# Scaling x by rows ahead of its transposes, and running the norm units eight at a time, in a hybrid attention layer step

## What is computed

```
mod = silu(c) @ w_ada + b_ada            # shift, scale, gate, for each of 9 batch entries
h = rmsnorm(x, ln_gain) * (1 + scale) + shift
proj = h @ w_in                          # q_a, ckv, krope, g_a, q_b, k_b, v_b, q_i, k_i, w_i, g_b
o_a = latent attention(q_a, ckv, krope)  # 8 heads, chunk-causal
o_b = sparse attention(q_b, k_b, v_b, top-k of an indexer on q_i, k_i, w_i)
y = concat(rmsnorm(o_a) * silu(g_a), rmsnorm(o_b) * silu(g_b))
out = rmsnorm(x + gate * (y @ w_out))    # and the new rows of the caches are outputs too
```

## Time and profile before

| | |
|---|---|
| median of 3 runs | 901.76 us (901.02 to 901.81) |
| profiled execution | 901.86 us |
| its span | 900.1 us |
| TensorE busy (matmuls) | 869.3 us, 97% |
| VectorE busy | 440.8 us, 49% |
| ScalarE busy | 335.4 us, 37% |
| DMA over the span | 190.07 MB, mean 211 GB/s |

### The profile page before, as it was taken

The page is one execution under the profiler, slowest core; times in us unless marked ns, Lnnn a source line. Parts: engine busy times, 40 slices in busy tenths (PEclk is TensorE's granted clock), DMA queues, the critical chain, the costliest instruction groups (busy, mean ns, idle before and its releaser), DMA issues.

```text
span 900.1 us, 14070 instructions
## 1 busy us (share of the span) xinstructions
PE 869.3 (97%) x5686; PEld 766.5 (85%) x5686; DVE 440.8 (49%) x910; ACT 335.4 (37%) x624; POOL 125.7 (14%) x207
## 2 busy tenths in 40 slices
PE   3998999999999999999999999999999999999996
PEld 2776778899999988888899989988999998888886
DVE  3523433443744314444455467364465466677262
ACT  3324334244443333332333354233244336554252
POOL 0000002110210000013241300000212123530000
PEclk9999999999999999999999999999999999999999
DMA  9999976855444334357463486655798733894313
GB/s 369 356 404 418 387 266 184 261 186 176 155 147 141 106 108 150 119 154 245 163 189 120 124 284 231 231 190 193 266 326 275 270 114 111 304 280 131 128 63 124
DMA packets 50352, 190.07 MB, mean 211 GB/s; under 512 B 7632, under 2 KB 8264, under 8 KB 45040
## 3 DMA queue, kind: packets, MB, share of 16 engines
q1 hardware_dynamic: 35280, 141.35, 44.2%
q0 software_dynamic: 14864, 47.30, 16.4%
q10 hardware_dynamic: 144, 0.52, 0.1%
HBM read 178.55 MB, written 12.69 MB: 212 GB/s over the span
## 4 chain that ended last, share of the span: by engine, by line
PE 89%; DVE 3%; ACT 3%; DMA 2%; issue 2%; SPq 0%; DVEq 0%; ACTq 0%
PE proj L2043 32%; PE proj L2033 30%; PE proj L2084 2%; PE bankO L2014 2%; PE proj L2014 2%; PE bankS L2043 1%; PE bankO L2168 1%; PE bankS L2084 1%; PE bankO L2180 1%; DMA araw<-in_ada_pairs 1%; PE bankT L2043 1%; DMA raw<-in_units 1%; PE bankO L2007 1%; PE bankS L2237 1%; ACT w_hi L1080 1%
## 5 line engine op out<-in xcount | busy, mean ns | idle before, releaser
L1449 DVE TENSOR_TENSOR w_lo<-raw,w_hi 128x1024 fp32r<-128x1024 f32 (+3 forms) x166 | 195.9, 1186 | 214.1 <-ACT w_hi L1080 213.0
L1080 ACT ACTIVATE w_hi<-raw 128x1024 fp32r<-128x1024 f32 (+3 forms) x168 | 168.3, 1006 | 169.5 <-PE proj L2033 92.6
L2043 PE MATMUL proj<-hT_hi,w_hi 128*128 128x384 f32 x576 | 198.0, 344 | 0.0
L2043 PE MATMUL proj<-hT_hi,w_lo 128*128 128x384 f32 x576 | 193.0, 335 | 0.0
L2043 PE MATMUL proj<-hT_lo,w_hi 128*128 128x384 f32 x576 | 192.8, 335 | 0.0
L2033 PE MATMUL proj<-w_hi,hT_hi 128*128 128x512 f32 (+2 forms) x458 | 174.4, 381 | 3.7 <-DVE hT_lo L1542 2.6
L2033 PE MATMUL proj<-w_hi,hT_lo 128*128 128x512 f32 (+2 forms) x458 | 171.3, 374 | 0.0
L2033 PE MATMUL proj<-w_lo,hT_hi 128*128 128x512 f32 (+2 forms) x458 | 171.1, 374 | 0.0
L2043 PEld LDWEIGHTS proj<-hT_hi,w_hi 128*128 128x128 f32 x576 | 108.2, 188 | 9.3 <-issue 7.7
L2043 PEld LDWEIGHTS proj<-hT_lo,w_hi 128*128 128x128 f32 x576 | 108.2, 188 | 0.1
L2043 PEld LDWEIGHTS proj<-hT_hi,w_lo 128*128 128x128 f32 x576 | 108.1, 188 | 0.0
(11 more groups left out here) (403 smaller groups left out, 1181.8 us busy)
## 6 DMA issues: line engine op xcount, KB each, us to landing
raw<-in_units SPq DMA_DIRECT2D x181, 512.0 KB, 4.0
araw<-in_ada_pairs SPq DMA_DIRECT2D x32, 1024.0 KB, 8.6
wuvT<-in_w_uv_t POOLq DMA_DIRECT2D x8, 512.0 KB, 6.7
kcT<-in_dsa_k_t POOLq DMA_DIRECT2D x8, 512.0 KB, 6.0
vc<-in_cache_dsa_v POOLq DMA_DIRECT2D x8, 512.0 KB, 5.1
gate_scratch<-stage POOLq DMA_DIRECT2D x8, 384.0 KB, 4.0
raw<-in_units SPq DMA_DIRECT2D x8, 336.0 KB, 3.5
raw<-in_units SPq DMA_DIRECT2D x8, 320.0 KB, 4.9
```

Of the source, the lines that this page charges most:

```text
L1080: return nc.scalar.activation(out, in_, func, scale=scale, **kw)
L1449: V.tensor_tensor(w_lo[:, SLOT[u], 0:w], raw_of(u)[:, 0:w], high(u)[:, 0:w].bitcast(F32), ALU.subtract).then_inc(lo_ready, 1)
L2043: ins = mm(banks[blk][:, 0:TOK], w[:, n, cols], a[:, kt, :], start=first and n == m == 0, stop=final and n == per - 1 and m == 2)
```

## The change

x is scaled in place by its row factors before it is turned: ScalarE takes columns 0 to 1023, VectorE 1024 to 2047, in three pieces each (`xs`). `rb`, `xdiag` and `rbc` are gone; the turns now wait for the scaled halves and go through x row tile by row tile (t = i // 4). The evictions of the turned blocks are plain copies, of bank T on VectorE and of bank S on ScalarE. Four turns stand behind unit 1, six behind unit 3, and the last two inside `first_unit`, ahead of row tile 2; `first_unit` does tiles 0 and 1 pass by pass. The first splits (`w0`) move behind `modT` 0 on ScalarE and into `h` 0 on VectorE.

The unit list of the opening is written anew. `ah` 1 runs in two runs of four, `ada` 1 to 3 in two runs of eight each; two or three projection units stand between the runs, and two behind each turn (the turn's own unit included). At the units of `TURNS` ScalarE and VectorE do the turn's steps ahead of the splits that stand in the same row. `osq` 7 moves from the row of unit 166 to that of unit 165. All units keep their content; the steps that are placed by the end of `ada` 3 (`ld_small`, `ld_const`, `bias`, `ld_uvT` and so on) come one or two units earlier.

```
-    out = a + key[:1] + b[:2] + g0[:1] + b[2:5] + one + b[5:]
+    out = a + key[:1] + b[:4] + one + b[4:]
     b = of("ada", 1)
-    out += two[:1] + b[:4] + key[1:2] + b[4:7] + two[1:] + b[7:10] + g0[1:2] + b[10:13] + three + b[13:]
+    out += two[:1] + g0[:1] + b[:8] + key[1:2] + two[1:] + b[8:]
     b = of("ada", 2)
-    out += one_b[:1] + b[:4] + key[2:3] + b[4:8] + g0[2:3] + b[8:12] + key[3:4] + b[12:14] + one_b[1:] + b[14:]
+    out += g0[1:2] + three + b[:8] + key[2:3] + one_b + b[8:]
     b = of("ada", 3)
-    out += two_b[:1] + b[:4] + key[4:5] + b[4:7] + g0[3:4] + b[7:10] + key[5:6] + b[10:13] + two_b[1:] + b[13:]
-    out += g1[:1] + key[6:] + g0[4:] + g1[1:] + g2
+    out += g0[2:3] + key[3:4] + b[:8] + key[4:5] + two_b[:1] + key[5:6] + b[8:]
+    out += g0[3:4] + two_b[1:] + key[6:] + g1[:1] + g0[4:] + g1[1:] + g2
...
-    put(0, ("xsq", 0), ("xsq", 1), ("xsq", 2), ("xr", 0))
-    put(1, ("rb", 0))
-    for n in range(6):
-        put(1 + n + 3 * (n > 4), ("xT", n), ("xS", n))
+    put(0, ("xsq", 0), ("xsq", 1), ("xsq", 2), ("xr", 0), ("xs", 0), ("xs", 1), ("xs", 2))
+    for n, u in enumerate((1, 1, 3, 3, 3)):
+        put(u, ("xT", n), ("xS", n))
 
     for n, ch in enumerate(MODS):
         u = LAST_UNIT[ch] + (n > 0)
         if n == 0:
-            put(u, ("w0", 0), ("busy", 1), ("modT", 0), ("busy", 5))
-            put(u + 1, ("h", 0), ("hl", 0), ("w1", 0))
+            put(u, ("busy", 1), ("modT", 0), ("w0", 0), ("busy", 5))
+            put(u + 1, ("h", 0), ("hl", 0), ("w1", 0), ("xT", 5), ("xS", 5))
...
-    run(u, "osq", 8)
+    run(u, "osq", 7)
+    put(u + 6, ("osq", 7))
...
+        def xs(t):
+
+            act.wait_ge(sem("x_rstd"), 1)
+            half = x_sb[:, t, 0:D // 2]
+            copy(half, half, scale=stat[:, 12 + t:13 + t]).then_inc(sem("x_lo_scaled"), 1)
+
+        def xS(n):
+
+            t, g = (2 * n + 1) // 4, (2 * n + 1) % 4
+            filled(act, "xS", n)
+            copy(xsT[:, 4 * g:4 * g + 4, P * t:P * (t + 1)],
+                 bank["S"][:].rearrange("p (k q) -> p k q", q=P)).then_inc(free["S"], 1)
...
-            copy(high(FIRST)[:, 512:UCOL], raw_of(FIRST)[:, 512:UCOL]).then_inc(hi_ready, 1)
...
+                copy(high(FIRST)[:, 512:UCOL], raw_of(FIRST)[:, 512:UCOL]).then_inc(hi_ready, 1)
...
-            for v in splits(u):
-                split(v)
+            if u not in TURNS:
+                for v in splits(u):
+                    split(v)
             if last_unit(u) and CHUNKS[c][0] not in ("wo", "gate"):
                 evict(c, u)
             for name, n in PLAN[u]:
                 if name in steps:
                     steps[name](n)
+            if u in TURNS:
+                for v in splits(u):
+                    split(v)
...
-            link(V.reciprocal(stat[:, 12:15], stat[:, 12:15]))
-            dve.wait_ge(sem("eye_in"), 16)
-            for t in range(NT):
-                V.tensor_scalar(xdiag[:, t, :], eye[:], stat[:, 12 + t:13 + t], None,
-                                ALU.mult).then_inc(sem("xs_ready"), 1)
-
-        def rb(n):
-            filled(dve, "rb", n)
-            V.tensor_copy(rbc[:], bank["S"][:, 0:TOK]).then_inc(free["S"], 1)
-
-        def turned(kind, n, b, i):
-
-            t, g = i % NT, i // NT
-            emptied(dve, "rb", 0)
-            filled(dve, kind, n)
-            V.tensor_tensor(xsT[:, 4 * g:4 * g + 4, P * t:P * (t + 1)], bank[b][:].rearrange("p (k q) -> p k q", q=P),
-                            rbc[:, P * t:P * (t + 1)].unsqueeze(1).broadcast_to([P, 4, P]),
-                            ALU.mult).then_inc(free[b], 1)
+            V.reciprocal(stat[:, 12:15], stat[:, 12:15]).then_inc(sem("x_rstd"), 1)
+
+        def xs(t):
+
+            dve.wait_ge(sem("x_rstd"), 1)
+            half = x_sb[:, t, D // 2:D]
+            V.tensor_scalar(half, half, stat[:, 12 + t:13 + t], None, ALU.mult).then_inc(sem("x_hi_scaled"), 1)
 
         def xT(n):
-            turned("xT", n, "T", 2 * n)
-
-        def xS(n):
-            turned("xS", n, "S", 2 * n + 1)
+
+            t, g = 2 * n // 4, 2 * n % 4
+            filled(dve, "xT", n)
+            V.tensor_copy(xsT[:, 4 * g:4 * g + 4, P * t:P * (t + 1)],
+                          bank["T"][:].rearrange("p (k q) -> p k q", q=P)).then_inc(free["T"], 1)
...
-        def w0(_):
-            dve.wait_ge(hi_ready, 1)
-            V.tensor_tensor(w_lo[:, SLOT[FIRST], 0:512], raw_of(FIRST)[:, 0:512], high(FIRST)[:, 0:512].bitcast(F32),
-                            ALU.subtract).then_inc(lo_ready, 1)
-
         def h(m):
 
             dve.wait_ge(sem("mod_ready"), m + 1 if m < 2 else m // 2 + 2)
-            emptied(dve, "xT", 5 if m > 1 else 1)
-            emptied(dve, "xS", 5 if m > 1 else 0)
+            emptied(dve, "xT", 5 if m > 1 else 4)
+            if m > 1:
+                emptied(dve, "xS", 5)
             if m == 0:
 
                 for kt in range(2):
-                    ins = V.tensor_scalar(h_first[:, kt, :], xsT[:, kt, 0:SEQ], modT[:, 1, kt, 0:1],
-                                          modT[:, 0, kt, 0:1], ALU.mult, ALU.add)
-                link(ins)
-                for kt in range(2):
-                    if kt:
-                        dve.wait_ge(hi_ready, 2)
-                        V.tensor_tensor(w_lo[:, SLOT[FIRST], 512:UCOL], raw_of(FIRST)[:, 512:UCOL],
-                                        high(FIRST)[:, 512:UCOL].bitcast(F32), ALU.subtract).then_inc(lo_ready, 1)
+                    links[0] += 1
+                    V.tensor_scalar(h_first[:, kt, :], xsT[:, kt, 0:SEQ], modT[:, 1, kt, 0:1],
+                                    modT[:, 0, kt, 0:1], ALU.mult, ALU.add).then_inc(chain, 1)
+                    dve.wait_ge(hi_ready, kt + 1)
+                    cols = slice(512 * kt, 512 * (kt + 1))
+                    V.tensor_tensor(w_lo[:, SLOT[FIRST], cols], raw_of(FIRST)[:, cols], high(FIRST)[:, cols].bitcast(F32),
+                                    ALU.subtract).then_inc(lo_ready, 1)
+                    dve.wait_ge(chain, links[0])
...
-            for t, n in ((0, 0), (1, 0), (0, 1), (1, 1), (2, 0), (2, 1)):
-                rows = slice(P * t, P * (t + 1))
-                if t == 0:
-                    pe.wait_ge(sem("hT_hi_ready"), n + 1)
-                    pe.wait_ge(hi_ready, n + 1)
-                if t == 2:
-                    pe.wait_ge(sem("hT_hi_ready"), 2 + MORE)
-                mm(banks[t][:], hT_hi[:, n, rows], hi_[:, n, :], start=n == 0, stop=False)
-                if t == 0:
-                    pe.wait_ge(lo_ready, n + 1)
-                mm(banks[t][:], hT_hi[:, n, rows], lo_[:, n, :], start=False, stop=False)
-                if t == 0:
-                    pe.wait_ge(sem("hT_ready"), n + 1)
-                if t == 2:
-                    pe.wait_ge(sem("hT_ready"), 2 + MORE)
-                ins = mm(banks[t][:], hT_lo[:, n, rows], hi_[:, n, :], start=False, stop=False)
+            for tiles in ((0, 1), (2,)):
+                if 2 in tiles:
+                    xT(5)
+                    xS(5)
+                for n in range(2):
+                    whole = MORE if 2 in tiles else 0
+                    pe.wait_ge(sem("hT_hi_ready"), (2 if whole else n + 1) + whole)
+                    for a, w, start in ((hT_hi, hi_, n == 0), (hT_hi, lo_, False), (hT_lo, hi_, False)):
+                        if w is lo_:
+                            pe.wait_ge(lo_ready, n + 1)
+                        elif a is hT_lo:
+                            pe.wait_ge(sem("hT_ready"), (2 if whole else n + 1) + whole)
+                        else:
+                            pe.wait_ge(hi_ready, n + 1)
+                        for t in tiles:
+                            ins = mm(banks[t][:], a[:, n, P * t:P * (t + 1)], w[:, n, :], start=start, stop=False)
...
-        def rb(n):
-            pe.wait_ge(sem("xs_ready"), NT)
-            mm(take("rb", n, "S")[:, 0:TOK], ones[:], xdiag[:].rearrange("p t q -> p (t q)"), start=True,
-               stop=True).then_inc(full["S"], 1)
-
         def turn(kind, n, b, i):
 
-            t, g = i % NT, i // NT
-            pe.wait_ge(sem(f"x_in{t}"), 16)
+            t, g = i // 4, i % 4
+            pe.wait_ge(sem("x_lo_scaled" if g < 2 else "x_hi_scaled"), t + 1)
```

More of the change, by code:

```diff
@@ L594, in program @@
     c_cols = at("c_cols", 80, [P, 9 * KT])
-    xdiag = at("xdiag", 82, [P, NT, P])
-    rbc = at("rbc", 86, [P, TOK])
     relb = at("relb", 88.5, [P, HEADS])
@@ L1166, in h @@
             act.wait_ge(sem("mod_ready"), m + 1 if m < 2 else m // 2 + 2)
-            emptied(act, "xT", 5 if m > 1 else 1)
-            emptied(act, "xS", 5 if m > 1 else 0)
+            emptied(act, "xT", 5 if m > 1 else 4)
+            if m > 1:
+                emptied(act, "xS", 5)
             if m == 0:
@@ L1364, in kl @@
                  bank["T"][:].rearrange("p (h s) -> p h s", s=P)).then_inc(free["T"], 1)
```

(8 more changed lines are left out.)

1 line of the change is left out of this document (added), and 2 rows, old and new, of the table STEP_BANKS.

## The result

The changed kernel takes **908.64 us** (median of five, 906.07 to 911.13) against 901.76 us before: ratio 1.0079, 95% interval 1.0056 to 1.0101. It is slower, as forecast, but by 6.9 us and not by 1.8, and it is 2.1 us above the wide range of the forecast (899.5 to 906.5) and 3.1 above its own (901.7 to 905.5). The profiled execution is the slowest of the five (911.13 us, span 909.3), so single times from it lie up to 2.5 us late by the end. The five executions also differ more than those of the kernel before do, and their mean granted clock goes with it: 0.994 to 0.995 in the two shortest, 0.987 to 0.990 in the other three.

A forecast was written before the change was run, and what follows sets the result against it. TensorE bounds the kernel, with DMA nearly even in the opening; -1.9 - 2.5 - 3.5 + 8.6 + 2.7 - 1.5 = +1.9, along the path +1.8 us: 903.6 us, own range 901.7 to 905.5, wide 899.5 to 906.5.

The forecast's parts named there:

- the price of the waits: New `araw` waits inside runs of eight, counted at 8.6 and 2.7 us, with usual unit lengths behind them.
- TensorE slows after the waits: Rival: each of three or four new waiting stretches brings a slow start of 1 to 1.5 us; 907 to 909 us; chance 0.08.
- Unit 10 ends at 34.8, 1.9 us earlier: Opening, up to the second unit of `ah` 1: the scaled x saves 1.9 us (bounds 1.0 and 2.9).
- x is scaled beside other work: Opening: scaling done by 17.3 us on ScalarE and 16.8 on VectorE, beside the first norm units and turns.
- New waits of 8.6 and 2.7 us for `araw`: Runs of eight: 8.6 us of waits up to `ada` 2 k8, then 2.4 to 3.1 more, taken as 2.7.
- The hole and the pair of `ada` 3 k6: Load queue dry near 87 to 91 us; that pair lands 17.5 to 18.2 us after the run's start, wanted at 15.1.
- The old waits at the turns, -3.5 us: Turns: steps ahead of the splits remove TensorE's waits, 2.6 us for `hT_lo` and 0.85 for `modT`.
- `osq` 7, -1.5 us: Near 530 us: the last square one row earlier removes TensorE's 1.51 us wait for `ysum` (bounds 0 and -1.5).
- TensorE's own work behind unit 10, -2.5 us: Behind unit 10: fewer separate norm runs and fewer projection units following them save 2.5 us (bounds 1.4 and 3.2).
- The rate, 0.41 MB/us: Loads in the opening move at 0.4095 MB/us, against 0.49 asked by a cycle with a run of eight.

The follow-up runs named there:

- the kernel with filled gaps: The changed kernel plus 38 small products of ones ahead of the nine norm-unit pairs where TensorE waited: 904.74 us, ratio 1.0029.
- the kernel with eight places ahead: The changed kernel with projection loads put eight places ahead of their units in the load order instead of six (`AHEAD` 8): 898.79 us, ratio 0.9963.
- the two halves above: Two runs: the changed kernel with the old unit list, 898.32 us; the kernel before with the new unit list alone, 909.88 us.
- the new order only: The kernel before with the new unit list and nothing else of the change: 909.88 us, ratio 1.0096.
- the edit alone: The kernel before with only the turn's steps put ahead of the splits on ScalarE and VectorE: 900.69 us, ratio 0.9984.
- the kernel with half columns: The changed kernel, loading only half of each norm unit's columns on all 128 partitions from each slot's second use on: 892.41 us, ratio 0.9891.

## Why the prediction was right in its sign and wrong in its size

The forecast was 903.6 us, the result 908.64: 5.0 us. **The step that failed is the price of the waits.** The sum put a wait for `araw` at its own length and the products behind it at their usual lengths, and the clock at nothing. The mechanism was named, as the rival "TensorE slows after the waits", with 907 to 909 us, and given a chance of 0.08. It was the right one: filled gaps gave 3.9 us back, and the kernel with filled gaps, 904.74, is 1.1 us from the forecast.

That the rival's figure holds 908.64 is in part luck: it counted three or four places of 1 to 1.5 us, from the first 32 matmuls, whose windows show the clock at 1.00; measured were two places of 2.9 us in the slowest execution, at 0.50.

The argument against the rival was that the waits of up to 1.5 us at the turns had no slow unit behind them. At the turn near 70 us of the kernel before they read:
```profile
71.91 1.93 PE L2014 MATMUL bankO<-araw,cs 128*32 128x256 f32 x32 [0.85 <-DVE modT L1497]
75.34 0.47 PE L2033 MATMUL proj<-w_hi,hT_hi 128*128 128x512 f32 x1 [1.50 <-DVE hT_lo L1542]
```
Those were two waits, 0.85 and 1.50 us, with 1.93 us of matmuls between them, and the granted clock stayed at 1.00 (TensorE busy 5.65 of the 8 us from 70 to 78). A run of eight gives two or three waits of up to 1.4 us with 1.1 us of small matmuls between them, and there the clock fell in most cases, though not in all: TensorE was busy 2.87 of 5 us at 45 to 50, where the clock fell to 0.86 on the mean, and 1.93 of 5 us in the kernel with eight places ahead of its stretch at 0.66. The prediction took one harmless case for the rule. Its own numbers said that the new waits are another case: some 8.6 us in three runs whose norm units take 0.43 us each. That should have given the rival far more than 0.08, or a term in the sum: 2.9 us at a place (0.9 for two norm units and 2.0 for the `kb` unit).

The prediction named the Trainium skill ("TensorE: Matmul & The Clock Gate", Part 1) for this rival: idle time brings the low rate, and sustained work wins back the full one. The trace agrees in that the price was paid behind the waits (6.33 us for 4.33 at a clock of 0.50 to 0.63). That waits this short, with matmuls between them, are enough is what these runs add.

Point by point:

- *Unit 10 ends at 34.8, 1.9 us earlier*: right. It ended at 34.7 or so, though the first landing was 0.35 us later than in the kernel before. Alone the scaled x is worth some 1.6 us. Its lead moved the landing of `ada` 2 k6 forward too, as the path of the prediction had it, and was lost behind that (see the two halves above).
- *x is scaled beside other work*: right; 17.4 and 16.3 us against 17.3 and 16.8. VectorE took 0.69 us for 1024 columns, less than the bound of 0.96. `modT` 0 came 1.6 us earlier, for 1.7.
- *New waits of 8.6 and 2.7 us for `araw`*: right in sum, 11.0 measured for 11.3, and the landing of `ada` 2 k6 at 76.46 for 76.2. This is the mechanism and no luck: by 76.46 us 29.1 MB were moved (381 GB/s), for the 29.35 worked out. From the same landing the prediction counted 11.8 us to `ada` 2 k8; it took 14.6, of which 2.9 are the two slow pieces.
- *The hole and the pair of `ada` 3 k6*: right in kind. The hole is at 87 to 92 us, for 87 to 91. The pair landed at 110.65, 19.6 us behind the run's start for 17.5 to 18.2. SyncE's three issues of projection loads took 3.12 us there where one usually takes 0.43, and the three pairs behind them 1.87 for 1.0 (0.33 each), so this pair was issued 2.7 us later than by the usual durations. Two other runs bear on it: with filled waits the last pair was issued 4.1 us behind the run's start and landed at 18.4, with the new order only 5.0 and 18.5; here it was 5.9 and 19.6. That fits, but no run changed only the issues.
- *The old waits at the turns, -3.5 us*: the waits went. With the old order the edit alone gave 1.6 us, since 1.0 us of waits for `araw` came in their place: the loads were even with TensorE before the change, as the first part of the prediction says. In the new order the waits for loads are a term of their own, and the kernel with half columns fits the full 3.5.
- *`osq` 7, -1.5 us*: 1.2 us by its median, the wait gone: right within the error.
- *TensorE's own work behind unit 10, -2.5 us*: not tested apart. The kernel with half columns, which is the change without its waits, came out at 892.41 for the 892.4 worked out, so the terms of saved work hold in sum; errors that cancel between them are not ruled out.
- *The rate, 0.41 MB/us*: right; 405 to 429 GB/s in the windows shown in which the queue was full. No wait was taken away by a higher rate.

What the prediction did not ask at all is whether `LOADS` still fits the new unit list. `AHEAD` was left at 6 by the change, and that alone is 9.9 us.

## What to carry to other kernels

When a run of small work outpaces its loads, look at three things apart: the waits (11.0 us here), the slow matmuls behind repeated short waits (3.9 us by the medians), and the place of each load in the queue, which decides how many of both there are (`AHEAD` 8 took away 4.2 us of waits and most slow matmuls, 9.9 us in all). When the order of the work is written anew, write the order of the loads anew with it: the best kernel here has the old order of units, the rest of the change and loads eight places ahead, 897.48 us, 0.52% under the kernel before; with loads six places ahead it is 898.32 and can't be told from it. Before taking a wait away, look what is nearly late behind it: of 2.9 us of waits taken at the turns 1.6 came out at the end. And before filling a gap, measure one filling product: at 0.26 us for an assumed 0.06 the filling outlasted the gap.

## What the runs showed of the hardware

- The granted clock was 0.50 behind two waits of 1.39 and 1.41 us with 1.07 us of matmuls between them (72.6 to 76.5 us), and the `kb` unit behind took 6.33 us for 4.33. The kernel before had waits of 0.85 and 1.50 us with 1.93 us between them, kept its clock at 1.00, and had no such unit.
- The lengths of the waits alone don't decide it. In `ada` 3 of the same execution the pair behind waits of 1.39 and 1.42 us still took 1.07 us, and the clock fell behind a third wait. With the new order only, waits of 0.24, 1.42 and 1.41 us ended in a slow pair (1.93 us) in `ada` 1, and waits of 0.21, 1.42 and 1.41 us in none (1.07 us) in `ada` 3. What decides between them stays open.
- In five executions of one kernel the mean clock varied from 0.987 to 0.995 and the time by 5.1 us; with the gaps filled, the clock was 0.998 in all six and the time varied by 1.1 us.
- A stretch in which the norm pairs went to 64 partitions (and the projection loads to 128) moved 243 GB/s with the DMA engines full; the kernel after, all on 128 partitions, moved 393 in the same stretch. The Trainium skill ("SBUF — State Buffer", "Door 1: The DMA port swizzle") says that partitions 0 to 63 reach half of the ports and gives some 218 GB/s for them. The mean here, with loads to all partitions among them, is a little above that and agrees.
- Halving the columns to 2 KB a row on all partitions left room in the DMA engines (share 0.82).
- SyncE's three issues of projection loads behind the hole took 3.12 us, for some 0.43 each in the kernel before; the same three took 1.59 us in the kernel with filled gaps and 2.26 with the new order only. What makes them longer stays open.
- A product of ones by ones (128 columns, float32) is two matmuls in the trace and takes 0.26 us at the full clock.
